# ALPHA x joins the expert rows where they leave PSUM, and two combines sum two gated rows only

## The chip, the cores and the metric

The kernel runs on one core of one Trainium2 chip. The metric is the device time of one execution in microseconds (us). The engines are TensorE (PE, with its weight loads as PEld), VectorE (DVE), ScalarE (ACT), GpSimd (POOL) and SyncE (SP); the last three and the DMA queues also start transfers. All data here are float32.

## What is computed

The reference is one step of a two-layer decoder for 1024 prompt tokens and 8 sample tokens, 1032 rows of D = 1024. Each layer has a mixer (layer 0: RWKV-7 heads and windowed attention; layer 1: causal pooling) and a mixture of 16 experts, of which each token uses two. After both comes a residual with ALPHA and a layer norm:

```python
gates = vals / vals.sum(-1, keepdims=True)          # the two gates of a token sum to 1
for e in range(N_EXPERTS):
    h = jax.nn.silu(xt @ w_gate[e]) * (xt @ w_up[e])
    y = y + dense_gate[:, e:e + 1] * (h @ w_down[e])
...
x = layer_norm(ALPHA * x + h, ln_mix_g, ln_mix_b)   # after the mixer
f = moe_ffn(x, ...)
x = layer_norm(ALPHA * x + f, ln_ffn_g, ln_ffn_b)   # after the experts
```

## The kernel before

The kernel is a row of stages, one after the other, with a barrier of all engines between them: projection and attention, the recurrence, the output projection of layer 0, then twice an expert stage and a combine. Line numbers are those of the kernel before.

**Expert stage** (`experts`, once for each layer). Tokens are sorted by expert into blocks of 128 slots; 22 blocks are worked through in layer 0 and 24 in layer 1. Block j is handled in body j of a loop that every engine runs, two bodies (u = 0, 1) to an iteration; buffers are double, chosen by u. In body j TensorE does, in this order, the gate and up products of block j (L2390), the transposes of the x rows of block j+1 (L2362), the down products of block j-1 (L2373) into PSUM banks 5 and 6, and the transposes of hidden of block j (L2402). ScalarE does Silu (L2455), half of the copy of the transposed x (`xT`, L2435), then `out` for block j-1: columns 0 to 511 of the result from PSUM to `y` (L2445), the start of the store of `y` to `slots_out` in DRAM (L2448); and last the copy of the transposed hidden (`hiddenT`, L2460). VectorE does the product of hidden and up (L2583), the other half of `xT` (L2435), and columns 512 to 1023 of the result (L2578). GpSimd gathers the x rows of block j+1 into `xs` (`ex_x_rows`, L2336) once the transposes of block j-1 have freed the buffer. SyncE loads the experts' weights, 3 MB each. The semaphores that matter: `xt` (x transposed), `ya` and `yv` (the two halves of `y`), `s_st` (a store has landed), `hc` (hiddenT copied), `down_plus_1` (down products done, plus one).

**Pooling combine** (`combine_pool_mix`, stage `cm`, between the layers). It goes over nine tiles of tokens, the tile of 8 samples first. For each tile GpSimd gathers the two expert rows of every token; ScalarE multiplies the first by its gate (L1731); VectorE adds the second with its gate (L1785), adds ALPHA x (L1787), and does the norm in five passes (L1821 to L1848). TensorE then does the band products of the pooling (L1665), a product with the weights (L1682) with ALPHA x added by a matmul with ALPHA times the identity (L1680), and, after a second norm on VectorE, transposes and router products. A step of the loop handles four tiles at different depths: VectorE's second norm of tile s-2, the first of tile s+1; TensorE's band of tile s, products of tile s-1, transposes of tile s-3.

**Final combine** (`combine`, stage `cb`, the end of the kernel). For each of the nine tiles TensorE sums three terms into PSUM: ALPHA x by a matmul with ALPHA times the identity (L2645), and each of the two gathered rows by a matmul with a diagonal matrix of its gates (L2647), for each half of the columns. Each float32 matmul stands as two instructions in the trace. ScalarE makes the diagonals, those of tile i+2 after the root of tile i (L2660). VectorE does the norm of each tile from PSUM, SyncE stores it. Four tiles fit in PSUM.

## Time and profile before

| | us |
|---|---|
| median of 3 runs | 1603.74 |
| lowest and highest | 1598.55, 1604.15 |
| the profiled execution | 1602.93 |
| its span, first to last instruction | 1601.1 |
| TensorE busy | 1440.0 (90%) |
| VectorE busy | 647.0 (40%) |
| ScalarE busy | 365.1 (23%) |
| GpSimd busy | 210.8 (13%) |
| mean granted TensorE clock | 0.932 |

The busy times are means over stages with different limits. The profile also gives a chain of waits, followed back from the last instruction; tables of busy time by stretch, with the clock that TensorE was granted (1.00 is the upper of its two levels, 0.50 the lower); a timeline, in which the brackets at a row's end give the idle time of the engine before it and what ended that; and the packets of each DMA queue in a stretch.

### The profile page before, as it was taken

How to read it: one execution, taken by the hardware profiler on the slowest of the kernel's cores; microseconds unless marked ns; L12 is line 12 of the kernel's file. 1: busy time of each engine (PE TensorE's matmuls, PEld its weight loads, DVE VectorE, ACT ScalarE, POOL GpSimd, SP SyncE). 2: the span in 40 equal slices, each digit the busy share in tenths (PEclk: the TensorE clock that was granted, in tenths of full speed). 3: DMA queues.
4: the chain of work that ended last, by engine and by line, in shares of the span. 5: the costliest groups of instructions: out<-in, count | busy, mean ns of one | idle time of the engine just before them, and what ended most of it. 6: DMA issues, size and time to landing. Idle time of an engine off the chain costs nothing. (4 is left out here: it accounts for less than half of the span.)

```text
span 1601.1 us, 26296 instructions
## 1 busy us (share of the span) xinstructions
PE 1440.0 (90%) x10111; PEld 880.7 (55%) x10112; DVE 647.0 (40%) x1046; ACT 365.1 (23%) x790; POOL 210.8 (13%) x266
## 2 busy tenths in 40 slices
PE   6999999999689998999479999985993799999968
PEld 4666666666588884445234444433983344444423
DVE  1014443367367753866621111115886111111127
ACT  1004444442323321111111111111221111111111
POOL 4000000000434412110010101005000110101040
PEclk8999998999789999999779999995897899999988
DMA  8593000000210013101667888756025788876353
GB/s 205 119 392 131 15 17 23 27 1 0 58 34 4 5 31 117 40 27 57 215 227 271 302 277 303 269 178 224 1 83 184 249 297 279 292 271 227 126 227 117
DMA packets 137055, 236.96 MB, mean 148 GB/s; under 512 B 20178, under 2 KB 100035, under 8 KB 136682
## 3 DMA queue, kind: packets, MB, share of 16 engines
q1 hardware_dynamic: 113458, 151.01, 29.7%
q0 software_dynamic: 16880, 60.49, 10.2%
q10 hardware_dynamic: 6624, 24.12, 3.7%
q8 instruction: 71, 1.16, 0.3%
q14 instruction: 22, 0.18, 0.0%
HBM read 178.92 MB, written 58.21 MB: 148 GB/s over the span
## 5 line engine op out<-in xcount | busy, mean ns | idle before, releaser
L2390 PE MATMUL ex_pb<-ew_w_gate_up,ex_xT 128*128 x736 | 329.1, 600 | 6.2 <-issue 3.7
L502 PE MATMUL pj_pb<-pj_xT,pj_w 128*128 128x348 f32 (+3 forms) x960 | 293.7, 462 | 0.8 <-ACT pj_xT L536 0.8
L502 PEld LDWEIGHTS pj_pb<-pj_xT,pj_w 128*128 128x128 f32 (+1 forms) x960 | 178.1, 188 | 104.2 <-issue 10.0
L2390 PEld LDWEIGHTS ex_pb<-ew_w_gate_up,ex_xT 128*128 128x128 f32 x736 | 137.7, 192 | 164.6 <-issue 163.7
L2373 PE MATMUL ex_pb<-ew_w_down,ex_hiddenT 128*128 x368 | 165.7, 593 | 3.4 <-ACT ex_hiddenT L2460 3.4
L2583 DVE TENSOR_TENSOR ex_hidden<-ex_hidden,ex_pb 128x256 f32<-128x256 f32 x46 | 19.4, 422 | 323.8 <-ACT ex_hidden L2455 323.8
L2373 PEld LDWEIGHTS ex_pb<-ew_w_down,ex_hiddenT 128*128 128x128 f32 x368 | 66.3, 190 | 69.9 <-issue 69.9
L2578 DVE COPY ex_y_rows<-ex_pb 128x512 f32<-128x512 f32 x46 | 31.8, 692 | 134.5 <-PE ex_pb L2373 134.5
L2455 ACT ACTIVATE ex_hidden<-ex_pb 128x256 f32<-128x256 f32 x46 | 17.8, 386 | 260.6 <-PE ex_pb L2390 260.6
L813 DVE SCALAR_TENSOR_TENSOR mixed<-pj_pb,v_mu,mixed 128x347 f32<-128x347 f32 (+3 forms) x42 | 24.0, 572 | 123.0 <-ACT mixed L655 123.0
L2333 POOL COPY ex_tokens_now<-ex_token_of_slot 128x1 uint32 (+1 forms) x48 | 9.6, 201 | 450.3 <-PE ex_pb L2362 398.7
L2362 PEld LDWEIGHTS ex_pb<-k_ident,ex_x_rows 128*128 128x128 f32 x384 | 46.3, 145 | 36.9 <-issue 24.2
L2362 PE MATMUL ex_pb<-k_ident,ex_x_rows 128*128 128x128 f32 x384 | 51.6, 279 | 12.4 <-DMA ex_x_rows<-scratch_x_stored,ex_tokens_now 12.4
L655 ACT ACTIVATE mixed<-pj_pb,pj_one_minus_mu 128x347 f32<-128x347 f32 (+3 forms) x42 | 23.0, 547 | 167.9 <-PE pj_pb L502 167.9
L1990 PE MATMUL mo_pb<-late_rows,projected_qkv 128*128 128x512 f32 x128 | 59.7, 610 | 0.0
L2445 ACT COPY ex_y_rows<-ex_pb 128x512 f32<-128x512 f32 x46 | 27.0, 586 | 136.7 <-PE ex_pb L2373 136.7
L1990 PE MATMUL mo_pb<-mo_w,minus_kk_then_y 128*128 128x512 f32 x128 | 58.1, 593 | 0.0
L2336 POOL DMA_INDIRECT ex_x_rows<-scratch_x_stored,ex_tokens_now x48 | 46.5, 969 | 38.1 <-POOL ex_tokens_now L2333 38.1
L1990 PEld LDWEIGHTS mo_pb<-late_rows,projected_qkv 128*128 128x128 f32 x128 | 25.1, 197 | 31.5 <-issue 31.5
L1682 PE MATMUL cm_pb<-pm_w_pool,cm_pooled 128*128 128x256 f32 (+1 forms) x144 | 41.5, 415 | 0.0
L1990 PEld LDWEIGHTS mo_pb<-mo_w,minus_kk_then_y 128*128 128x128 f32 x128 | 23.6, 190 | 26.3 <-issue 26.3
L2435 ACT COPY ex_xT<-ex_pb 128x512 f32<-128x512 f32 x48 | 28.1, 586 | 38.7 <-PE ex_pb L2362 38.7
(423 smaller groups left out, 2025.4 us busy)
## 6 DMA issues: line engine op xcount, KB each, us to landing
ew_w_gate_up<-in_w_ex_gate SPq DMA_DIRECT2D x32, 1024.0 KB, 6.6
ew_w_gate_up<-in_w_ex_up SPq DMA_DIRECT2D x32, 1024.0 KB, 9.5
ew_w_down<-in_w_ex_down SPq DMA_DIRECT2D x32, 1024.0 KB, 12.5
scratch_slots_out<-ex_y_rows ACTq DMA_DIRECT2D x46, 512.0 KB
scratch_slots_out<-pj_tmp POOLq DMA_DIRECT2D x4, 4096.0 KB
scratch_x_stored<-x_rows SPq DMA_DIRECT2D x16, 512.0 KB
pj_w<-in_w_in SPq DMA_DIRECT2D x7, 1024.0 KB, 8.7
minus_kk_then_y<-in_x_prompt SPq DMA_DIRECT2D x8, 512.0 KB, 5.5
```

The source lines that it names most:

```text
L502: last = nc.tensor.matmul(product(at)[:, 0:tn], w[:, k_slab % NW, k, c0:c0 + mrows], xT[:, k, x0:x0 + tn], start=(k == 0), stop=(k == KD - 1))
L655: nc.scalar.activation(pr[0:mrows, tile, t0:t0 + n], product(at)[:, 1:1 + n], ACT.Identity, scale=omu[0:mrows, tile:tile + 1]).then_inc(s_ ...
L813: last = stt(out=out[:, 0:n_prompt], in0=product(at)[:, 0:n_prompt], scalar=mu, in1=out[:, 0:n_prompt], op0=ALU.mult, op1=ALU.add)
L1682: last = mm(at, feats[:, j % 2, 2 * gi + k, 0:n], pm.w[:, 2 * gi + k, :], start=False, stop=(k == 1))
L1990: last = mm(pb[0:n, 2 * (i % 2) + h, :], lhs(k, i), (w[:, k, 512 * h:512 * h + 512] if k < 4 else w_swa[:, k - 4, 512 * h:512 * h + 512]), ...
L2336: pool.indirect_dma_start(xs[:, u, :], None, io["x_stored"], bass.IndirectOffsetOnAxis(ap=now[:, u:u + 1], axis=0)).then_inc(s_xs[u], 16)
L2362: last = nc.tensor.transpose(pb[:, k // 4, P * (k % 4):P * (k % 4) + P], xs[:, u, P * k:P * k + P], const["ident"][:, :])
L2373: last = mm(pb[:, 5 + half, :], hT[:, u, k, :], w[:, k, 512 * half:512 * half + 512], start=(k == 0), stop=(k == 1))
L2390: last = mm(pb[:, 2 + u, :], xT[:, u, k, :], w[:, k, :], start=(k == 0), stop=(k == KD - 1))
L2435: copy(xT[:, u, 4 * half:4 * half + 4, :], pb[:, half, :].rearrange("p (k t) -> p k t", k=4)).then_inc(q[sem], 1)
L2445: nc.scalar.copy(y[:, u, 0:512], pb[:, 5, :]).then_inc(q["ya"], 1)
L2578: nc.vector.tensor_copy(y[:, u, 512:1024], pb[:, 6, :]).then_inc(q["yv"], 1)
```

## The change

In the expert stage ScalarE first writes ALPHA x of the block's rows into the result's buffer `y`, and VectorE adds both PSUM banks of the down products to it in one instruction of 1024 columns. The stored rows are then ALPHA x + expert(x). Since a token's two gates sum to 1, the gated sum of its two stored rows holds ALPHA x already, and both combines leave that term out. ScalarE's pass waits until the rows are there (`s_xs`) and until the last store from that buffer has landed (`s_st`); this last wait stood at the result copies before. GpSimd's gather waits for the pass too (`alpha_x`), since the pass reads the rows that the gather overwrites.

```diff
@@ combine_pool_mix, VectorE
-                stt(out=r1, in0=r2, scalar=gates[0:n, i, 1:2], in1=r1, op0=ALU.mult, op1=ALU.add).then_inc(q["both"], 1)
-                dve.wait_ge(q["both"], j + 1)
-                stt(out=x_(j), in0=x_(j), scalar=ALPHA, in1=r1, op0=ALU.mult, op1=ALU.add).then_inc(qa["res"], 1)
+                stt(out=x_(j), in0=r2, scalar=gates[0:n, i, 1:2], in1=r1, op0=ALU.mult, op1=ALU.add).then_inc(qa["res"], 1)
@@ experts, GpSimd, before the gather of block j+1
                     pool.wait_ge(q["xt"], j)
+                    pool.wait_ge(q["alpha_x"], j)
@@ experts, TensorE, before the down products
-                        pe.wait_ge(q["ya"], j - 1)
-                        pe.wait_ge(q["yv"], j - 1)
+                        pe.wait_ge(q["y"], j - 1)
@@ experts, ScalarE
             def out(i, u, first):
                 j = 2 * i + u
-                act.wait_ge(q["down_plus_1"], j + 2)
-                if not first:
-                    act.wait_ge(s_st[u], 16 * i)
-                nc.scalar.copy(y[:, u, 0:512], pb[:, 5, :]).then_inc(q["ya"], 1)
-                act.wait_ge(q["ya"], j + 1)
-                act.wait_ge(q["yv"], j + 1)
+                act.wait_ge(q["y"], j + 1)
                 act.dma_start(io["slots_out"][bass.ds(j * P, P), :], y[:, u, :]).then_inc(s_st[u], 16)
             def body(i, u, first):
                 j = 2 * i + u
+                act.wait_ge(s_xs[u], 16 * i + 16)
+                if not first:
+                    act.wait_ge(s_st[u], 16 * i)
+                nc.scalar.activation(y[:, u, :], xs[:, u, :], ACT.Identity, scale=ALPHA).then_inc(q["alpha_x"], 1)
                 act.wait_ge(q["gu"], j + 1)
@@ experts, VectorE, out
                 dve.wait_ge(q["down_plus_1"], j + 2)
-                if not first:
-                    dve.wait_ge(s_st[u], 16 * i)
-                nc.vector.tensor_copy(y[:, u, 512:1024], pb[:, 6, :]).then_inc(q["yv"], 1)
+                dve.wait_ge(q["alpha_x"], j + 1)
+                nc.vector.tensor_tensor(y[:, u, :], y[:, u, :], pb[:, 5:7, :].rearrange("p b n -> p (b n)"), ALU.add)\
+                    .then_inc(q["y"], 1)
@@ combine, TensorE
-            pe.wait_ge(q["alpha"], 1)
...
-                    nc.tensor.matmul(out[0:n, h, :], alpha_i[0:n, 0:n], xr[0:n, i, half], start=True, stop=False)
                     for c in range(2):
                         last = nc.tensor.matmul(out[0:n, h, :], diag[0:n, i % 2, c, 0:n], r[0:n, i, c, half],
-                                                start=False, stop=(c == 1))
+                                                start=(c == 0), stop=(c == 1))
@@ combine, ScalarE
-            nc.scalar.activation(alpha_i[:, :], const["ident"][:, :], ACT.Identity, scale=ALPHA).then_inc(q["alpha"], 1)
```

On ScalarE one body of the expert loop of the kernel before reads as follows, from Silu (`ex_hidden`) to the copy of `hiddenT`; `ex_y_rows` is `y`, and the DMA is the store to `slots_out`.

```order
L2455 ACTIVATE ex_hidden<-ex_pb 128x256
L2433 REGISTER_ALU
L2435 COPY ex_xT<-ex_pb 128x512
L2444 REGISTER_ALU
L2445 COPY ex_y_rows<-ex_pb 128x512
L2448 ISA
L2448 DMA scratch_slots_out<-ex_y_rows 128x1024
L2460 COPY ex_hiddenT<-ex_pb 128x256
```

The same body of the changed kernel, on the same engine (`ex_x_rows` are the gathered rows; line numbers are those of the changed kernel):

```order
L2447 ACTIVATE ex_y_rows<-ex_x_rows 128x1024
L2451 ACTIVATE ex_hidden<-ex_pb 128x256
L2430 REGISTER_ALU
L2432 COPY ex_xT<-ex_pb 128x512
L2440 ISA
L2440 DMA scratch_slots_out<-ex_y_rows 128x1024
L2456 COPY ex_hiddenT<-ex_pb 128x256
```

The pass that writes `y` now stands ahead of Silu, and the copy from PSUM between `xT` and the store is gone from this engine.

On VectorE a steady step of the pooling combine begins as follows in the kernel before: the second norm of one tile (`cm_stats_b`), then the gated sum and the first norm of a later one (`cm_stats_a`).

```order
L1821 BN_STATS cm_stats_b<-cm_pb 128x6 x2
L1824 BN_AGGR cm_stats_b<-cm_stats_b 128x2
L1831 SCALAR_TENSOR_TENSOR x_rows<-cm_pb,cm_stats_b,late_rows 128x1024
L1785 SCALAR_TENSOR_TENSOR cm_expert_rows<-cm_expert_rows,gates 128x1024
L1787 SCALAR_TENSOR_TENSOR x_rows<-x_rows,cm_expert_rows 128x1024
L1821 BN_STATS cm_stats_a<-x_rows 128x6 x2
```

And in the changed kernel:

```order
L1819 BN_STATS cm_stats_b<-cm_pb 128x6 x2
L1822 BN_AGGR cm_stats_b<-cm_stats_b 128x2
L1829 SCALAR_TENSOR_TENSOR x_rows<-cm_pb,cm_stats_b,late_rows 128x1024
L1785 SCALAR_TENSOR_TENSOR x_rows<-cm_expert_rows,gates 128x1024
L1819 BN_STATS cm_stats_a<-x_rows 128x6 x2
```

One pass of 128 x 1024 is gone between the two norms; the rest stands as it did.

## Rows read from the trace of the kernel before

**Rows 1.** The page's chain that ended last, by line, shares of the span.

```profile
PE cb_pb L2647 2%; PE cb_pb L2645 1%; DMA cb_expert_rows<-scratch_slots_out,slots 0%; DVE cb_stats L1821 0%; DVE x_rows L1848 0%; DVE x_rows L1831 0%; POOL cb_expert_rows L2621 0%; DVE cb_stats L1824 0%; POOL cb_eps L2617 0%; DVE cb_stats L1845 0%; POOLq L119 0%
```

**Rows 2.** Busy time by stretch; columns as in its first line.

```profile
core 0: us, PE busy (x) PEld busy (x) DVE busy (x) ACT busy (x) POOL busy (x), PEclk, DMA share, GB/s
830.00:1060.00 230.00, 230.00 (x684) 112.04 (x683) 35.64 (x60) 38.62 (x80) 21.78 (x38) 1.00 0.81 283
...
1112.00:1132.00 20.00, 20.00 (x62) 11.58 (x61) 11.50 (x15) 2.90 (x5) 0.00 (x0) 0.50 0.02 6
1146.30:1190.20 43.90, 43.62 (x328) 39.64 (x328) 42.78 (x61) 14.16 (x24) 0.00 (x0) 1.00 0.01 1
1208.40:1217.00 8.60, 4.42 (x55) 3.62 (x53) 4.48 (x9) 2.74 (x5) 0.00 (x0) 1.00 0.15 61
1544.50:1548.30 3.80, 3.80 (x5) 1.73 (x6) 0.00 (x0) 0.00 (x0) 2.89 (x4) 0.50 0.97 353
1552.00:1593.30 41.30, 41.30 (x96) 16.52 (x94) 33.13 (x48) 7.74 (x23) 5.97 (x7) 0.99 0.49 194
```

**Rows 3.** Timeline of one body of the expert loop, layer 0: start, duration, instruction, idle before.

```profile
910.26 0.34 ACTq L2448 DMA_DIRECT2D scratch_slots_out<-ex_y_rows  x1
...
916.50 0.39 ACT L2455 ACTIVATE ex_hidden<-ex_pb 128x256 f32<-128x256 f32 x1 [5.48 <-PE ex_pb L2390]
...
917.30 0.69 DVE L2435 COPY ex_xT<-ex_pb 128x512 f32<-128x512 f32 x1
...
918.42 0.96 POOL L2336 DMA_INDIRECT ex_x_rows<-scratch_x_stored,ex_tokens_now  x1 [0.81 <-POOL ex_tokens_now L2333]
...
920.75 7.03 PE L2390 MATMUL ex_pb<-ew_w_gate_up,ex_xT 128*128 x16
...
920.83 0.69 DVE L2578 COPY ex_y_rows<-ex_pb 128x512 f32<-128x512 f32 x1 [2.84 <-PE ex_pb L2373]
```

**Rows 4.** Prices: the instructions of L1787, and the timeline row of L1731.

```profile
L1787 DVE SCALAR_TENSOR_TENSOR x_rows<-x_rows,cm_expert_rows x9: 1214/1224/1226, 1089.9 to 1183.2; 128x1024 f32<-128x1024 f32 x8, 8x1024 f32<-8x1024 f32 x1
...
1164.27 1.13 ACT L1731 ACTIVATE cm_expert_rows<-cm_expert_rows,gates 128x1024 f32<-128x1024 f32 x1
```

**Rows 5.** ScalarE's DMA queue: packets, MB, from 1310.2 to 1317.5; then 1533 to 1535.4.

```profile
q10 hardware_dynamic: 142, 0.52, 17.4%
...
q10 hardware_dynamic: 144, 0.52, 54.2%
```

**Rows 6.** Timeline around those two stores, and at the end of the pooling combine.

```profile
1216.92 0.17 DVE L1795 COPY logits<-cm_pb 128x16 f32<-128x16 f32 x1 [2.46 <-PE cm_pb L1709]
1218.44 0.40 SPq L2229 DMA_DIRECT2D ew_w_gate_up<-in_w_ex_gate  x1
...
1310.30 0.34 ACTq L2448 DMA_DIRECT2D scratch_slots_out<-ex_y_rows  x1
...
1533.10 0.34 ACTq L2448 DMA_DIRECT2D scratch_slots_out<-ex_y_rows  x1
1537.09 0.10 POOL L2617 MEMSET cb_eps<- 128x1 f32 x1 [34.86 <-POOLq L119]
```

**Rows 7.** Timeline: the last down products of the expert stage of layer 0.

```profile
1071.26 3.70 PE L2373 MATMUL ex_pb<-ew_w_down,ex_hiddenT 128*128 x8 [1.72 <-ACT ex_hiddenT L2460]
```

**Rows 8.** Timeline of the pooling combine: the ramp on ScalarE, a steady step on TensorE.

```profile
1104.33 0.21 ACT L1747 COPY cm_pooled<-cm_pb 128x64 f32<-128x64 f32 x1 [10.28 <-PE cm_pb L1661]
...
1179.25 0.30 PEld L1665 LDWEIGHTS cm_pb<-pm_band,x_rows 128*128 128x128 f32 x2 [0.16 <-DVE x_rows L1848]
```

**Rows 9.** Timeline of VectorE in the final combine.

```profile
1551.88 1.30 DVE L1821 BATCH_NORM_STATS2 cb_stats<-cb_pb 128x6 f32<-128x512 f32 x2 [19.02 <-PE cb_pb L2647]
...
1555.32 1.28 DVE L1848 SCALAR_TENSOR_TENSOR x_rows<-x_rows,cb_stats,late_rows 128x1024 f32<-128x1024 f32 x1
...
1556.95 1.30 DVE L1821 BATCH_NORM_STATS2 cb_stats<-cb_pb 128x6 f32<-128x512 f32 x2 [0.35 <-issue]
...
1559.92 1.28 DVE L1848 SCALAR_TENSOR_TENSOR x_rows<-x_rows,cb_stats,late_rows 128x1024 f32<-128x1024 f32 x1
...
1596.29 1.27 DVE L1848 SCALAR_TENSOR_TENSOR x_rows<-x_rows,cb_stats,late_rows 8x1024 f32<-8x1024 f32 x1
```

More of the change, by code:

```diff
@@ L1605, in combine_pool_mix @@
         qb = {k: m.sem(f"b_{k}") for k in LN}
-        q = {k: m.sem(k) for k in "eps alpha sel first both wscaled band feats tr cp rp rpc rl ev zero keep".split()}
+        q = {k: m.sem(k) for k in "eps alpha sel first wscaled band feats tr cp rp rpc rl ev zero keep".split()}
         s_r = [m.sem(f"rows{i}") for i in range(TILES)]
@@ L2275, in experts @@
         r = {k: m.sem(f"route_{k}") for k in "mx ex as rk chain lanes blocks sum parts part tokens token_list now tokens_set tab".split()}
-        q = {k: m.sem(k) for k in "gu xt down_plus_1 ht silu h xca xcv hc ya yv loaded stored".split()}
+        q = {k: m.sem(k) for k in "gu xt down_plus_1 ht silu h xca xcv hc alpha_x y loaded stored".split()}
         s_xs = [m.sem(f"x_rows{u}") for u in range(2)]
@@ L2426, in _ @@
             c = entry(pe, 2 * final + (T_SETS + 1), 0, SETS - 1)
-            pe.wait_ge(q["ya"], 2 * final + 1)
-            pe.wait_ge(q["yv"], 2 * final + 1)
+            pe.wait_ge(q["y"], 2 * final + 1)
             down(final, 1, c)
@@ L2600, in combine @@
         diag = m.sb("gate_diagonals", [P, 2, 2, P])
-        alpha_i = m.sb("alpha_ident", [P, P])
         st = m.sb("stats", [P, 2, 18])
@@ L2604, in combine @@
         pb = m.psum("pb", [P, 8, 512])
-        q = {k: m.sem(k) for k in "eps alpha diag res st var root rs g x out".split()}
+        q = {k: m.sem(k) for k in "eps diag res st var root rs g x out".split()}
         s_r = [m.sem(f"rows{i}") for i in range(TILES)]
```

## The prediction

> **What bounds the kernel now.** I read the page's chain of waits first: its end is TensorE alone, in the last stage, the final combine [rows 1]. The table of stretches comes next, since the change touches three kinds of stage. In the expert loops TensorE is busy for 230.00 of 230.00 us at full clock, with VectorE at 36 and ScalarE at 39 us [rows 2]: whatever VectorE and ScalarE do there is free as long as TensorE is not kept waiting. In the steady part of the pooling combine both TensorE (43.62 of 43.9 us) and VectorE (42.78) are full [rows 2], so relief for one of them alone is worth little. In the final combine TensorE is busy for 41.30 of 41.30 us and VectorE for 33.13 [rows 2]. There the reader should see one clear bound, and how near the second engine stands behind it.
>
> **Final combine.** The two alpha matmuls of a tile go; at f32 each is two instructions, so 12 become 8. 96 instructions in 41.30 us [rows 2] are 0.430 us each: TensorE needs 3.44 us for a tile in place of 5.16. VectorE is next. A tile whose data are there takes it from the statistics at 1556.95 to the end of the last pass at 1559.92 + 1.28 = 1561.20 [rows 9], 4.25 us, say 4.28 with the hop to the next tile. So the stage changes its bound and gains 0.9 us a tile, not 1.7. From the start: TensorE begins at 1544.5 as before, since both versions wait there for the gathered rows. Its first instructions run at clock 0.50 [rows 2], the later ones of the first tile at full clock; the four that go are the last four in time, 4 x 0.43 = 1.72 us, so the first statistics start at 1551.88 - 1.72 = 1550.16. The first tile takes 4.72 us on VectorE as before (a table load on ScalarE lies in it: 1551.88 to 1556.60 [rows 9]), the next seven 7 x 4.28 = 30.0, the last 4.2, in all 1589.1 in place of 1596.29 + 1.27 = 1597.56 [rows 9]: **-8.5 us**. Covers: TensorE has a tile ready 3.44 us after its diagonals, which ScalarE makes one tile ahead, so it keeps ahead of 4.28. The gathers are all issued before 1560, so rows come faster than either engine eats them. Had TensorE stayed the bound, the gain would be 9 x 1.72 = 15.5; that end I exclude by VectorE's 4.25.
>
> **Pooling combine.** VectorE loses one pass of 1.224 us on 128 x 1024 for each of nine tiles [rows 4], 11.3 us with hops. Nearly all of it is covered by TensorE. In the ramp ScalarE has idled 10.28 us for TensorE's first band products when it copies them at 1104.33 [rows 8], and from 1112 to 1132 TensorE is busy 20.00 of 20.00 us at clock 0.50 [rows 2]; only the very first tile's chain (gate, sum, norm) stands ahead of TensorE's start, so the whole ramp moves by one pass, -1.25. In the steady steps TensorE waits 0.16 us a step for VectorE's last pass [rows 8], five times: -0.8. The tail has no gathered tile in it. Sum **-2.05 us**, with about 1 us either way from the moment at which the clock rises, which need not move along with the work.
>
> **Expert loops.** Three edits. First, the result leaves PSUM in one VectorE add over 1024 columns, in place of two half copies side by side. It is not in the trace; its neighbours are 1.22 us (three operands, SBUF, [rows 4]) and 1.28 us [rows 9], so 1.25 against 0.69 [rows 3], and everything behind it comes 0.56 us later: the store, and ScalarE's copy of hiddenT, which is queued behind the store. Inside the loop TensorE needs hiddenT only after the next gate/up products (7 us), so this is free. At the end of a layer it is not: the last down products do wait for that copy, 1.72 us [rows 7], and then the last result itself is on the path. Two layers x 2 x 0.56 = **+2.2 us**.
>
> Second, ScalarE gets a pass ALPHA x over 128 x 1024, 1.13 us by the like pass of the pooling combine [rows 4]. ScalarE has idled 5.48 us before Silu at 916.50 [rows 3], so the pass itself fits. But a wait moves with it: y's buffer must be free, so the store of two blocks ago must have landed, and that wait now stands ahead of Silu, where before it stood behind. Queued behind it are Silu, VectorE's product and both copies of xT, and TensorE waits for these. In the block shown, the store is issued at 910.26 + 0.56 = 910.82. VectorE's xT copy ends at 917.99 and TensorE takes it at 920.75 [rows 3]; counted back over Silu and product, Silu may start as late as 919.1, so the pass must start by 917.9: **7.1 us** after the store's issue. What a store takes: a quiet one has its 144 packets through 2.3 us after issue, and its signal shows at most 4.0 us after issue (1533.10 to 1537.09), a hand-over between stages included [rows 5, 6]. Such a hand-over without a transfer is 1217.09 to 1218.44, 1.35 us [rows 6], so the signal comes about 0.35 us after the last packet. Under the weights' traffic the slowest store, issued at 1310.30, has 142 of 144 packets through by 1317.5 [rows 5, 6]. Followed in this way, the 46 stores take 2.3 to 7.5 us, middle about 4.3. With 0.35 us for the signal four of them pass the limit, by 1.8 us in all, or by near nothing if the later issue does not delay the landing. I take **+1 us**; the ends are 0 and, if the whole 1.7 us between last packet and next stage were the signal's own, about 20 us (17 stores over 5.4 us). I stand near the low end because the hand-over has a measured price.
>
> Under load the signal's delay is in no row. The Trainium skill (DMA: Bandwidth & Descriptors, "Latency and other measured facts") gives an HBM access as 0.2 us on average and 2 us at high load, and says that this receipt makes most of a transfer's fixed cost. By its 2 us the limit would be passed by about 27 us in all; the quiet rows here agree with its low figure, and no row shows its high one.
>
> Third, GpSimd's gather into x's buffer waits for the ALPHA x pass as well as for the transposes. The gather at 918.42 [rows 3] fetches the rows that are transposed two blocks after, near 939; even if the pass ends at 919 it starts 1.6 us later and keeps over ten. Free. SP's queue is not moved past anything.
>
> **Sum** against the profiled execution, 1602.93 us (span 1601.1): -8.5 - 2.05 + 2.2 + 1 = -7.35, which gives 1595.6. The median of the runs lies 0.8 above that execution, so on its scale I say **1596**. The covered cases end at 1592 (no store passes, early clock) and 1601 (several more do).
>
> **Rivals.** (a) The wait for the store takes the gain: slower. Mechanism: ScalarE stands at the ALPHA x pass until a late store signals, Silu is late, TensorE idles. It decides from a signal 7.1 us after issue; with 1.7 us between packets and signal it costs 20 us, so 1602.9 - 8.5 - 2.05 + 2.2 + 20 = 1614.6. For it: the slowest stores are already at 7.5 us [rows 5]. Against it: the 0.35 us of quiet stores. Chance 0.14, part of it with a small bill, between 1601 and 1611.
>
> (b) The clock falls in the final combine: slower. TensorE would work 3.44 us and idle 0.84 in every tile. At clock 0.50 a tile costs 8 x 0.86 = 6.9 us, above VectorE's 4.28, and the stage ends at 1544.5 + 9 x 6.9 + 4.2 = 1610.8 in place of 1597.6, so the kernel at 1602.9 + 13.2 - 2.05 + 3.2 = 1617. Against it: at the end of the pooling combine TensorE is busy 4.42 of 8.60 us, half the time, and the clock stays at 1.00 [rows 2]. Chance 0.05. The Trainium skill (TensorE: Matmul & The Clock Gate, "A second HAM failure mode: psum-queue depth-cycling") tells of a kernel whose short idles between groups of matmuls made the clock swing between its two levels, which speaks for this rival; the row at half load speaks against it.
>
> (c) VectorE, not TensorE, sets the step in the pooling combine, and most of the 11.3 us are gained: about 1602.9 - 8.5 - 10 + 3.2 = 1588. For it: TensorE does wait for VectorE in each step. Against it: only 0.16 us [rows 8]. Chance 0.08.
>
> **Chances.** Forecast 0.68, (a) 0.14, (b) 0.05, (c) 0.08, something else 0.05. The range 1591 to 1607 leaves out (b), the dear half of (a) and most of (c). 0.5% of 1603.74 is 8.0 us, about what a measurement of this kernel tells from no change; the forecast lies 0.3 us inside it. So a little under half of the forecast (0.30), (c) and a share of the rest say faster: 0.40. The other part of the forecast and the small bills of (a) say no change: 0.46. Slower: 0.14.
>
> **What would show it.** Final combine: VectorE's statistics every 4.28 us without idle time, TensorE's matmuls in groups of eight with gaps, clock 1.00, and 44.5 us from the first matmul to the last pass in place of 53.1. Pooling combine: no wait of TensorE for x_rows in the steady steps, step 10.8 us in place of 10.97. Expert loops: no TensorE wait for xT or hidden, except in a few blocks. The ends of both layers 1.1 us longer. I am wrong if TensorE idles for ScalarE or VectorE in many blocks, if a clock of 0.50 shows after 1552 in the final combine, or if the pooling steps shrink by a microsecond.

## The result and the profile after

| | before | changed |
|---|---|---|
| median | 1601.14 us (1597.94 to 1604.15, 4 runs) | 1653.37 us (1650.16 to 1667.18, 4 runs) |
| ratio, 95% interval | | 1.0331 [1.0291, 1.0372] |
| span of the profiled execution | 1601.1 | 1654.5 |
| TensorE busy | 1440.0 | 1455.0 |
| VectorE, ScalarE busy | 647.0, 365.1 | 658.2, 382.7 |

The kernel is 3.3% slower; the forecast was 1596 us. The first thing to do with such a result is to cut both spans at the same events: SyncE's first load of expert weights in each layer, and the memsets of `cm_eps` and `cb_eps` that open the two combines. In brackets stands how long TensorE's clock was granted at 0.50 in that stage.

| stage, us | before | changed | difference | forecast |
|---|---|---|---|---|
| ahead of the experts | 783.2 (64.3) | 790.2 (79.1) | +7.0 | 0 |
| experts, layer 0 | 296.9 (40.9) | 316.6 (47.0) | +19.7 | +1.6 |
| pooling combine | 138.4 (53.1) | 137.2 (55.3) | -1.2 | -2.05 |
| experts, layer 1 | 318.6 (38.8) | 354.7 (61.2) | +36.1 | +1.6 |
| final combine | 64.0 (19.6) | 55.7 (24.9) | -8.3 | -8.5 |

So the two combines did what was forecast, and the whole loss lies in the expert loops, +55.8 us where I had +3.2. (The first stage is the same code in both; it had 14.8 us more at clock 0.50, and half of that is its 7 us. All stage lengths, here and below, are read from one profiled execution of each kernel.)

The final combine, VectorE's timeline from the first tile on, answers to [rows 9]:

```profile
1612.94 1.29 DVE L1819 BATCH_NORM_STATS2 cb_stats<-cb_pb 128x6 f32<-128x512 f32 x2 [18.28 <-PE cb_pb L2640]
...
1617.59 1.29 DVE L1819 BATCH_NORM_STATS2 cb_stats<-cb_pb 128x6 f32<-128x512 f32 x2
...
1621.75 1.29 DVE L1819 BATCH_NORM_STATS2 cb_stats<-cb_pb 128x6 f32<-128x512 f32 x2
...
1649.63 1.27 DVE L1846 SCALAR_TENSOR_TENSOR x_rows<-x_rows,cb_stats,late_rows 8x1024 f32<-8x1024 f32 x1
```

Behind the first tile the statistics come every 4.16 us with no idle time in brackets: VectorE is the bound now, as forecast (4.28). The clock was granted at 1.00 from 1612.3 to 1643.0, while TensorE worked 3.67 of every 4.16 us. Then it fell, with half of the last tile still to do:

```profile
1643.00:1651.00 8.00, 2.92 (x4) 0.26 (x2) 7.69 (x12) 0.59 (x2) 0.00 (x0) 0.50 0.33 132
```

The eight matmuls of that tile took 4.98 us in place of 3.67, but VectorE came to it only at 1646.71, after their end, so it cost nothing. The stretches in the expert loop and in the steady part of the pooling combine answer to [rows 2] (stretch, its length, busy time and instructions of PE, PEld, DVE, ACT, POOL, then clock, DMA share, GB/s):

```profile
830.00:1060.00 230.00, 214.90 (x628) 103.29 (x626) 41.98 (x56) 42.48 (x74) 20.64 (x36) 0.99 0.75 261
1174.00:1217.00 43.00, 43.00 (x332) 39.42 (x331) 38.18 (x57) 13.44 (x23) 0.00 (x0) 1.00 0.06 22
```

In the pooling combine TensorE is full and VectorE has slack (38.18 of 43.00 where it had 42.78 of 43.90): the relief of VectorE is worth little there, as forecast. In the expert loop TensorE, which was busy for 230.00 of 230.00 us in the kernel before, has lost 15.1, and got 628 instructions done in place of 684. The page's group of the gate/up products, before and then changed (count, busy, mean ns of one, idle time before them and what ended most of it), says more:

```profile
L2390 PE MATMUL ex_pb<-ew_w_gate_up,ex_xT 128*128 x736 | 329.1, 600 | 6.2 <-issue 3.7
```

```profile
L2389 PE MATMUL ex_pb<-ew_w_gate_up,ex_xT 128*128 x736 | 344.7, 624 | 40.2 <-issue 28.4
```

Idle time ahead of these products went from 6.2 to 40.2 us, and the same 736 instructions are busy 15.6 us longer: 49.6 of the 55.8 us. Most of the idle time is ended by "issue", which is the profile's word for a wait that it cannot put to any other engine or DMA. One body of the loop, layer 0, shows how it comes about. First ScalarE and VectorE:

```profile
936.32 0.34 ACTq L2440 DMA_DIRECT2D scratch_slots_out<-ex_y_rows  x1
936.70 0.37 ACT L2456 COPY ex_hiddenT<-ex_pb 128x256 f32<-128x256 f32 x1 [4.73 <-DVE ex_y_rows L2573]
944.25 1.06 ACT L2447 ACTIVATE ex_y_rows<-ex_x_rows 128x1024 f32<-128x1024 f32 x1 [7.17 <-DMA scratch_slots_out<-ex_y_rows]
945.21 0.37 ACT L2451 ACTIVATE ex_hidden<-ex_pb 128x256 f32<-128x256 f32 x1
...
945.61 0.42 DVE L2579 TENSOR_TENSOR ex_hidden<-ex_hidden,ex_pb 128x256 f32<-128x256 f32 x1 [9.48 <-ACT ex_hidden L2451]
945.95 0.68 DVE L2432 COPY ex_xT<-ex_pb 128x512 f32<-128x512 f32 x1
```

The store goes out at 936.32, the ALPHA x pass can start at 944.25, Silu at 945.21; in [rows 3] Silu stood 6.24 us after the store's issue, here it stands 8.89. By 946.63 the last thing that TensorE's next products need (VectorE's half of `xT`) is there. TensorE itself:

```profile
946.09 0.44 PE L2400 MATMUL ex_pb<-k_ident,ex_hidden 128*128 128x128 f32 x2
949.51 8.82 PE L2389 MATMUL ex_pb<-ew_w_gate_up,ex_xT 128*128 x16 [2.98 <-issue]
```

The transposes of hidden run at 946.09, as soon as hidden is there (945.61 + 0.42 = 946.03). Then TensorE does nothing for 2.98 us, although all its data are in place 0.1 us after the transposes' end. And the products behind the idle time take 8.82 us where they take 7.03 in [rows 3]: the clock, which stood at 1.00, is granted at 0.58 in the mean from 949.5 to 953.0:

```profile
949.50:953.00 3.50, 3.49 (x5) 1.59 (x6) 0.00 (x0) 0.36 (x1) 0.00 (x0) 0.58 0.96 354
```

So the wait for the store is there, as rival (a) had it. But it does not explain 3 us with all data in place. The profile does show what TensorE's sequencer did in that time, if one asks for the lines of the loop and of the table reads and not for the matmuls. The reads of the table of blocks in the changed kernel, in the window 946 to 950 (count, lowest, middle and highest ns of one, first and last start; PEldq is TensorE's sequencer):

```profile
L2287 PEldq TENSOR_LOAD <-block_experts x3: 297/297/299, 946.9 to 948.3; - x3
```

The loop's own instructions stand from 946.09, 0.05 us after hidden is ready, to 946.68; the three reads and what goes with them from 946.73 to 948.93; the waits and the address of the weights from 948.99 to 949.45; and the first weight load at 949.50. The same three reads in the body of [rows 3], kernel before:

```profile
L2289 PEldq TENSOR_LOAD <-block_experts x3: 299/306/308, 917.5 to 918.9; - x3
```

Hidden is ready at 917.34 there, and the sequencer's first instruction behind the wait stands at 917.39; but the array is then still at the down products, until 920.5, so the reads cost nothing. In all 46 bodies of both kernels the sequencer's next instruction comes 0.05 us after hidden is ready.

**The theories.** A: TensorE's own stream stands at its wait for hidden, and what comes next in that stream, the loop's branch and three reads of the table of blocks (which expert, which set of weights), is done only after the wait; it costs about 3 us, which otherwise lie under the queued down products. The rows above speak for it; what a late Silu costs by it, and whether moving the reads takes the cost away, the runs below try. The order of TensorE's instructions in the kernel before, from the last down product into the next body (`block_experts` is the table, L2289 reads it):

```order
L2373 MATMUL ex_pb<-ew_w_down,ex_hiddenT 128x512
L2402 MATMUL ex_pb<-k_ident,ex_hidden 128x128 x2
L2289 ISA
L2289 TENSOR_LOAD block_experts
L2289 ISA x3
L2289 TENSOR_LOAD block_experts
L2289 ISA x2
L2289 TENSOR_LOAD block_experts
L2289 ISA x2
```

B: the lateness of the store, or the DMA traffic, is the whole cost. C: the ALPHA x pass itself is too much for ScalarE.

### The profile page after: what moved, and what is told of

The parts are those of the page before. It is cut to its first block and busy times, and to the rows that moved or that the text cites. A ratio compares the mean times of both kernels' runs of the same rounds, so it can differ in the third digit from the quotient of the medians.

```text
span 1654.5 us, 26187 instructions
## 1 busy us (share of the span) xinstructions
PE 1455.0 (88%) x10075; PEld 884.7 (53%) x10076; DVE 658.2 (40%) x1037; ACT 382.7 (23%) x789; POOL 211.8 (13%) x266
## 5 line engine op out<-in xcount | busy, mean ns | idle before, releaser
L2389 PE MATMUL ex_pb<-ew_w_gate_up,ex_xT 128*128 x736 | 344.7, 624 | 40.2 <-issue 28.4
L2389 PEld LDWEIGHTS ex_pb<-ew_w_gate_up,ex_xT 128*128 128x128 f32 x736 | 142.9, 199 | 211.5 <-issue 210.9
L2447 ACT ACTIVATE ex_y_rows<-ex_x_rows 128x1024 f32<-128x1024 f32 x46 | 48.7, 1058 | 193.0 <-DMA scratch_slots_out<-ex_y_rows 192.8
L2573 DVE TENSOR_TENSOR ex_y_rows<-ex_y_rows,ex_pb 128x1024 f32<-128x1024 f32 x46 | 56.1, 1220 | 93.5 <-PE ex_pb L2372 93.3
L2456 ACT COPY ex_hiddenT<-ex_pb 128x256 f32<-128x256 f32 x46 | 17.2, 373 | 173.6 <-DVE ex_y_rows L2573 173.6
L2640 PE MATMUL cb_pb<-cb_expert_rows,cb_gate_diagonals 128*128 128x512 f32 (+1 forms) x72 | 37.0, 666 | 15.6 <-DMA cb_expert_rows<-scratch_slots_out,slots 12.8
L2451 ACT ACTIVATE ex_hidden<-ex_pb 128x256 f32<-128x256 f32 x46 | 17.5, 380 | 98.0 <-PE ex_pb L2389 98.0
```

The costliest lines, as they stand in the source:

```text
L2389: last = mm(pb[:, 2 + u, :], xT[:, u, k, :], w[:, k, :], start=(k == 0), stop=(k == KD - 1))
L2447: nc.scalar.activation(y[:, u, :], xs[:, u, :], ACT.Identity, scale=ALPHA).then_inc(q["alpha_x"], 1)
L2573: nc.vector.tensor_tensor(y[:, u, :], y[:, u, :], pb[:, 5:7, :].rearrange("p b n -> p (b n)"), ALU.add)\
L2640: last = nc.tensor.matmul(out[0:n, h, :], diag[0:n, i % 2, c, 0:n], r[0:n, i, c, half], start=(c == 0), stop=(c == 1))
```

## Experiments

### The wait alone, the pass alone

`e1_wait_only` is the kernel before with one wait more:

```diff
             def body(i, u, first):
                 j = 2 * i + u
+                if not first:
+                    act.wait_ge(s_st[u], 16 * i)
                 act.wait_ge(q["gu"], j + 1)
```

> The kernel before, with one line more: in the expert loop ScalarE waits ahead of Silu until the store of two blocks ago has landed. No pass, no new add, combines as before. Theory (the wait for a late store holds back Silu): most of the loss of the two expert stages comes back, which was 56 us in the traces (316.6 + 354.7 us in place of 296.9 + 318.7); so about 1601 + 45 = 1646 us (the store starts 0.6 us earlier than in the changed kernel, so a little less than the whole). Rival (the pass, the longer add or the later gather cost the time): 1601 us, within 0.5%.

Measured: 1616.15 us, ratio 1.0083 [1.0048, 1.0119]. `e5_pass_only` has no wait for the store, but 1.24 us of useless work on ScalarE ahead of its wait for the gate/up products, into an unused PSUM bank:

```diff
+                for k in range(2):
...
+                    nc.scalar.activation(pb[:, 7, :].rearrange("p (k t) -> p k t", k=4),
+                                         const["ident"][:, :].unsqueeze(1).to_broadcast([P, 4, P]), ACT.Identity, scale=ALPHA).then_inc(q["own"], 1)
                 act.wait_ge(q["gu"], j + 1)
```

> The kernel before, with an extra pass of the same size on ScalarE ahead of Silu (two passes of 128 x 512 into an idle PSUM bank, unused, each waiting only for the one before on its own engine), and no wait for the store. Theory of the wait: ScalarE idles over 5 us there, so 1601 us within 0.5%. Rival (the pass itself): towards 1650 us.

Measured: 1602.28 us, 0.9996 [0.9967, 1.0025]. The gate/up group of e1, then of e5:

```profile
L2390 PE MATMUL ex_pb<-ew_w_gate_up,ex_xT 128*128 x736 | 331.2, 603 | 14.3 <-issue 11.6
```

```profile
L2390 PE MATMUL ex_pb<-ew_w_gate_up,ex_xT 128*128 x736 | 328.6, 600 | 6.2 <-issue 3.7
```

Theory C falls: a pass of this length that fits into ScalarE's idle time costs nothing. The wait alone costs 13 us, again by "issue", far less than the 45 us that I had expected of it. The other 43 come only with wait and pass together: the pass stands between the store's signal and Silu, and the stores of e1 land no later than those of the kernel before (4 of the 42 that are waited for have their last packet later than 6.75 us after issue, against 5).

### The pass behind Silu; the combines alone

`e3_pass_behind` is the changed kernel with both waits and the pass moved behind Silu and the copy of `xT`. `e4_combines_only` has the combines of the changed kernel and the experts of the kernel before; ALPHA x is left out of both residuals.

```diff
@@ e3, ScalarE (the same lines are gone from the start of body)
                 copy_x(act, nc.scalar.copy, 1 - u, 0, "xca", j + 1)
+                act.wait_ge(s_xs[u], 16 * i + 16)
+                if not first:
+                    act.wait_ge(s_st[u], 16 * i)
+                nc.scalar.activation(y[:, u, :], xs[:, u, :], ACT.Identity, scale=ALPHA).then_inc(q["alpha_x"], 1)
```

> The changed kernel, with ScalarE's ALPHA x pass and its wait for the store moved behind Silu and the copy of xT, and ahead of the start of the store. Same instructions, same sums. Theory of the wait ahead of Silu: the expert stages return to their length before, plus 1.1 us at the end of each; the combines keep their gain of about 9.6 us: 1601 - 9.6 + 2.2 = 1594 us. Rival (the pass, the add over 1024 columns or the gather's extra wait cost the time, wherever the pass stands): 1650 us as the changed kernel.

> The two combines of the changed kernel with the expert stage of the kernel before; ALPHA x is left out of both residuals. The part of the change that gains, alone. Expected from the stage lengths in the two traces (pooling combine -1.2, final combine -8.4): 1601 - 9.6 = 1591.5 us. If the combines' gain were only the other side of a later start, 1601 us.

Measured: e3 1602.41 us, 0.9996 [0.9966, 1.0025]; e4 1585.56 us, 0.9894 [0.9856, 0.9931]. Stages (clock 0.50 in brackets):

| stage, us | before | e4 | e3 |
|---|---|---|---|
| experts, layer 0 | 296.9 | 296.4 | 303.7 |
| pooling combine | 138.4 (53.1) | 127.1 (34.6) | 137.2 (55.3) |
| experts, layer 1 | 318.6 | 318.9 | 324.1 |
| final combine | 64.0 | 55.0 | 55.6 |

e4 is faster than forecast by 6 us, and not by the change: its pooling combine stood at clock 0.50 for 18.5 us less. Where that time is the same as before (e3, the changed kernel) the stage is 1.2 us shorter.

e3 takes 51 us off the changed kernel, so the place ahead of Silu is the loss. It still pays 12.5 us in the experts over e4. 2.2 are the ends of the layers; for the rest see the wait of TensorE's weight loads for gathered rows (total, times, longest), in e4 and then in e3:

```profile
PEld ex_pb L2360 <- DMA ex_x_rows<-scratch_x_stored,ex_tokens_now: 12.6, 2, 6.4
```

```profile
PEld ex_pb L2361 <- DMA ex_x_rows<-scratch_x_stored,ex_tokens_now: 29.7, 20, 6.4
```

The gather waits for the pass, and with the pass behind Silu it comes too late in 18 blocks, 17.1 us of waits at the weight loads. That is my third edit, which I had called free with over ten us of room. I had taken the wrong block: the gather of block j+1 waits for the pass of block j-1. In a steady body a gather was issued 20.7 us ahead of the transposes that need its rows in the kernel before, 9.2 to 17.6 us ahead in the changed kernel, and 5.6 to 9.1 us ahead in e3.

### What a late Silu costs, with no store in it

`e8_silu_late` is the kernel before with the same useless passes, this time between the wait for the gate/up products and Silu. Silu starts 1.53 us after the transposes of x in place of 0.28, so 1.25 us late in every block.

```diff
                 act.wait_ge(q["gu"], j + 1)
                 if not first:
                     act.wait_ge(q["ht"], j - 1)
+                for k in range(2):
...
+                    nc.scalar.activation(pb[:, 7, :].rearrange("p (k t) -> p k t", k=4),
+                                         const["ident"][:, :].unsqueeze(1).to_broadcast([P, 4, P]), ACT.Identity, scale=ALPHA).then_inc(q["own"], 1)
                 nc.scalar.activation(h[:, u, :], pb[:, 2 + u, 0:FF], ACT.Silu).then_inc(q["silu"], 1)
```

> The kernel before, with Silu made late by a fixed amount: ScalarE makes two useless passes of 512 columns behind its wait for the gate/up products, ahead of Silu, in each of the 46 blocks; about 1.2 us. No store is waited for. Theory A: the slack of Silu is under 1 us, so each block pays; with the 0.4 to 1.0 us a block that the stalls of the two earlier runs show for this lateness, 1620 to 1650 us. The slack of 2.6 us of my forecast: no cost, 1601 us.

Measured: 1654.2 us, 1.0309 [1.0286, 1.0332], just the size of the whole loss. Two bodies, TensorE's timeline:

```profile
933.42 0.38 PE L2402 MATMUL ex_pb<-k_ident,ex_hidden 128*128 128x128 f32 x2
934.20 7.13 PE L2390 MATMUL ex_pb<-ew_w_gate_up,ex_xT 128*128 x16 [0.39 <-issue]
...
945.47 0.38 PE L2402 MATMUL ex_pb<-k_ident,ex_hidden 128*128 128x128 f32 x2
946.89 7.13 PE L2390 MATMUL ex_pb<-ew_w_gate_up,ex_xT 128*128 x16 [1.03 <-issue]
```

and VectorE's product that makes hidden, in the same two:

```profile
931.04 0.42 DVE L2588 TENSOR_TENSOR ex_hidden<-ex_hidden,ex_pb 128x256 f32<-128x256 f32 x1 [9.34 <-ACT ex_hidden L2460]
...
943.02 0.42 DVE L2588 TENSOR_TENSOR ex_hidden<-ex_hidden,ex_pb 128x256 f32<-128x256 f32 x1 [8.61 <-ACT ex_hidden L2460]
```

Hidden is ready at 931.46 and 943.44. The transposes of hidden start no later than before (4.31 us after those of x), for they are queued behind the down products. What is late is the next body: its products start 2.74 and 3.45 us after hidden. The first is a body inside an iteration of the loop, the second crosses the loop's branch; all bodies of the run behind the first two of a layer alternate so, with periods (from one block's transposes of x to the next's) of 12.04 and about 12.7 us in place of 11.40 and 11.47. In the body of [rows 3], in the kernel before,

```profile
916.92 0.42 DVE L2583 TENSOR_TENSOR ex_hidden<-ex_hidden,ex_pb 128x256 f32<-128x256 f32 x1 [6.88 <-ACT ex_hidden L2455]
```

hidden is ready at 917.34, and 917.34 + 2.74 = 920.08 against a start at 920.75: a slack of 0.67 us. In bodies with the branch the slack is none (products 3.49 us after hidden, where 3.45 is the least); they last 11.47 and not 11.40 already in the kernel before. `e11_silu_half_as_late` has one useless pass in place of two, as a check on these two figures:

> The kernel before with one useless pass of 512 columns ahead of Silu in place of two, so Silu about 0.6 us late in every block. The run with two passes (1.26 us late) had periods of 12.04 and 12.71 us in turn, in place of 11.40 and 11.47, so a slack of 0.62 us in the blocks inside an iteration of the loop and of none in those at its branch. Expected by that: periods of 11.40 and about 12.1, 23 x 0.6 = 14 us in all, 1616 us. If the cost were proportional (0.94 us a block for 1.26 us), 22 us, 1624; if there were a threshold above 0.6 us, 1602.

Measured: 1622.14 us, 1.0093 [1.0068, 1.0119]. Silu is 0.54 to 0.59 us late, and the periods are 11.40 and 11.96 to 12.03 us, as expected: the bodies with slack pay nothing, the others nearly all. (The stages are 19.6 us longer, 6 more than expected: the way to the second body of each layer, where no down products cover TensorE's stream, pays 3.6 us.)

### TensorE's reads ahead of the wait

To try theory A itself, the transposes of hidden of block j, with their waits, stand behind the table reads of body j+1; the array executes the same instructions in the same order.

```diff
             def body(i, u, first):
                 c = entry(pe, T_SETS + j, 0, SETS - 1)
...
+                if not (first and u == 0):
+                    hidden_turned(i - 1 + u, 1 - u, first)
                 pe.wait_ge(q["xca"], j + 1)
...
                     down(i - 1 + u, 1 - u, c_before)
-                pe.wait_ge(q["h"], j + 1)
...
-                last.then_inc(q["ht"], 1)
```

On e8, `e9_silu_late_reads_first`:

> The same late Silu, with TensorE's transposes of hidden behind the table reads of the next body. Theory A: the slack is 2 to 3 us again, so 1.2 us cost nothing, 1602 us (1594 to 1610). Theory B: as without the move, 1620 to 1650 us.

Measured: 1608.91 us, 1.0033 [1.0012, 1.0054]; e8 without the move took 1654.2. Periods 11.40 us in every body behind the first two, with Silu as late as in e8, and the rows that answer to those of e8, TensorE's two and the reads of the table:

```profile
926.40 0.38 PE L2383 MATMUL ex_pb<-k_ident,ex_hidden 128*128 128x128 f32 x2
926.62 7.03 PE L2401 MATMUL ex_pb<-ew_w_gate_up,ex_xT 128*128 x16
```

```profile
L2289 PEldq TENSOR_LOAD <-block_experts x3: 298/302/305, 921.4 to 922.8; - x3
```

Hidden is ready at 924.44 there; the reads are over by 923.4 and no longer wait for it. (Its control, e7 below, takes 1591.34 us. In the profiled executions e9 has 7.7 us more in the experts, where the way to the second body of each layer takes 13.19 in place of 9.08 us, since no down products cover a late Silu there; and 7.7 us more in the pooling combine, with 18 us more at clock 0.50.)

On the changed kernel, `e6_reads_first`:

> The changed kernel, with one thing moved: TensorE's transposes of hidden of block j, and the waits for hidden ahead of them, stand at the start of body j+1, behind that body's reads of the table of blocks. What the array executes, and in which order, is unchanged. Theory A (a late hidden costs because TensorE's own stream stands at that wait and only then does the loop branch and the table reads, some 3 us, which otherwise lie under the queued down products): the slack of Silu grows to the 2 to 3 us of my forecast, TensorE idles behind the transposes of hidden in a few blocks only, and the time falls from 1653 to about 1597 us (1590 to 1610). Theory B (the lateness of Silu itself is the cost, or the memory traffic is): nothing changes, 1640 to 1655 us.

Measured: 1605.52 us, 1.0006 [0.9983, 1.0030], 48 us below the changed kernel. On the kernel before, as the control, `e7_reads_first_before`, and the same kernel once more beside the last runs, `e7_again`:

> The control: the same move of TensorE's transposes of hidden, on the kernel before. Silu is never late there, so theory A expects no change, 1601 us (1593 to 1609); if the move itself is worth something whatever Silu does, it shows here as 1590 us or less.

> The control again, on the same chip as the version in place: the kernel before with TensorE's transposes of hidden behind the table reads. 1591 us if its 12.6 us gain repeats (3.3 us of it in the expert loops, the rest in a shorter stretch at clock 0.50 in the pooling combine and ahead of the experts); 1599 us if that stretch is a matter of the run.

Measured: 1591.34 us, 0.9921 [0.9896, 0.9947], and 1593.53 us, 0.9930 [0.9904, 0.9956]. I had expected no change. Its experts are 2.3 and 0.8 us shorter (every body 11.40, none 11.47, and the second body of a layer 9.07 in place of 10.34); 7.3 us are the pooling combine, 131.1 (35.5 at clock 0.50) in place of 138.4 (53.1). So the 48 us between e6 and the changed kernel are not a gain that the move brings to any kernel: in the expert stages it takes 43.5 us off the changed kernel and 3.1 off the kernel before.

What e6 still pays is the store. Its experts take 300.9 and 326.9 us against 294.6 and 317.8 in the control, 15.4 us more; about 2 are the ends of the layers, and 12 bodies with a late Silu are 13.0 us over 11.40 in sum (in one of them about 0.9 us is a wait for late gathered rows). One of the two worst in layer 0:

```profile
928.91 1.06 ACT L2453 ACTIVATE ex_y_rows<-ex_x_rows 128x1024 f32<-128x1024 f32 x1 [7.83 <-DMA scratch_slots_out<-ex_y_rows]
...
930.83 0.43 PE L2382 MATMUL ex_pb<-k_ident,ex_hidden 128*128 128x128 f32 x2 [0.61 <-DVE ex_hidden L2585]
931.73 7.13 PE L2400 MATMUL ex_pb<-ew_w_gate_up,ex_xT 128*128 x16 [0.46 <-DVE ex_xT L2438]
```

Here TensorE's waits have names, hidden and xT, and no "issue". In e6 a body whose Silu is x us behind the transposes of x pays about x - 2.56: 3.11 gave 11.93 us, 4.39 gave 13.23, and 2.50 gave 11.40. Less the 0.28 at which Silu stands anyway, that is a slack of 2.3 us; I had counted 2.6.

### Waits taken out of Silu's way

`e12_pass_behind_reads_first` puts both cures together, the pass behind and the reads first:

> The changed kernel with the ALPHA x pass and its waits behind Silu and the copy of xT, and TensorE's transposes of hidden behind the table reads. With the pass behind, the experts took 303.7 and 324.1 us, against 296.4 and 318.9 without ALPHA x; the trace showed TensorE waiting for late gathers (11 us). If that is the rest of the cost, the move of the transposes gives only the 3 to 5 us it gave the kernel before: 1598 us. If the reads were the rest, 1590 us.

Measured: 1604.88 us, 1.0000 [0.9977, 1.0022], 7 us above what I had expected. The median is no better than that of e3. In the profiled execution its experts are 3.4 and 0.6 us shorter (300.3 and 323.5), and the late gathers stay: the waits of the weight loads for them are 30.9 us, 22 times. The rest of the cost of e3 is the gather.

`e10_in_place` takes the cause of both waits away. The result is written over the gathered rows, by one VectorE instruction that also applies ALPHA, and stored from there; the memory of the result's two buffers gives two more for gathered rows, and the wait for a landed store stands on GpSimd, four blocks later. With four buffers an iteration of the loop holds four bodies in place of two.

```diff
-        xs = m.sb("x_rows", [P, 2, D])
-        y = m.sb("y_rows", [P, 2, D])
+        xs = m.sb("x_rows", [P, 4, D])
@@ VectorE, out
+                nc.vector.scalar_tensor_tensor(out=at_(b), in0=at_(b), scalar=ALPHA,
+                                               in1=pb[:, 5:7, :].rearrange("p b n -> p (b n)"),
+                                               op0=ALU.mult, op1=ALU.add).then_inc(q["y"], 1)
@@ GpSimd, before the gather
                     pool.wait_ge(q["xt"], j)
-                    pool.wait_ge(q["alpha_x"], j)
...
+                    pool.wait_ge(s_st[1 - u], 16 * (i + u) - 16)
```

> The changed kernel with no pass and no wait ahead of Silu: the gathered rows have four buffers in place of two, the result's buffers are gone, and VectorE writes ALPHA x + down products over the gathered rows in one instruction of 1024 columns, from where they are stored. The wait for a landed store stands on GpSimd ahead of the gather four blocks on. TensorE's transposes of hidden stand behind the table reads, as in the two runs before. The combines are those of the changed kernel. Theory (both the lateness of Silu and the reads are cured, and the combines keep their gain): the control with the reads first (1591 us) less 8.4 us of the final combine and about 1 of the pooling combine, plus 2.2 at the ends of the layers: 1584 us (1578 to 1592). Rival (the saving in the combines is given back by something else that the fused rows bring): 1591 us or more.

Measured: 1595.2 us (1591.86 to 1598.58, 6 runs), 0.9932 [0.9915, 0.9949]. The gate/up group and the stretch of the expert loop:

```profile
L2408 PE MATMUL ex_pb<-ew_w_gate_up,ex_xT 128*128 x736 | 327.6, 598 | 3.6 <-DVE ex_xT L2446 3.0
```

```profile
830.00:1060.00 230.00, 229.99 (x685) 112.10 (x686) 46.29 (x60) 26.55 (x59) 22.74 (x39) 1.00 0.83 285
```

Nearly every body lasts 11.40 us, and the final combine keeps its gain (54.0 us). It is 8.8 us faster than the kernel before, and no faster than the kernel before with the reads first (1593.53 on the same chip). By the numbers that is the rival of my expectation. The stages of the profiled executions say where the gain of the final combine went: against e7_again that stage is 10.0 us shorter, but the experts are 3.3 and 2.2 longer, and the pooling combine 5.5, for it stood 54.6 us at clock 0.50 where the other stood 35.5. The first 60 us of the pooling combine in three kernels, the kernel before, e7_reads_first_before, and e10:

```profile
1080.00:1140.00 60.00, 42.11 (x185) 30.79 (x186) 37.31 (x45) 10.92 (x17) 22.78 (x23) 0.57 0.42 150
```

```profile
1076.00:1136.00 60.00, 40.17 (x236) 32.80 (x237) 45.36 (x57) 14.31 (x22) 22.79 (x23) 0.75 0.43 150
```

```profile
1083.00:1143.00 60.00, 43.33 (x191) 31.86 (x192) 33.68 (x44) 11.96 (x20) 22.47 (x23) 0.58 0.42 150
```

The mean clock of that stretch is 0.57, 0.75 and 0.58, and TensorE gets 185, 236 and 191 instructions done. In the profiled executions the time at 0.50 is near 35 us (e1, e4, both runs of e7), 42 (e5, e8, e11) or 54 (before, changed, e3, e6, e9, e10, e12). Only e7 has two such executions, and they agree; so even whether this belongs to the kernel or to the execution is open, and no run here was made for it.

## Why the prediction was wrong

**Final combine: right in its mechanism, and in its number with some luck.** -8.3 for -8.5; VectorE became the bound, and rival (b) did not come as far as VectorE had to wait for it: from the first matmul at 1606.09 to the end of the last pass at 1649.63 + 1.27 are 44.8 us (44.5 forecast). Two errors meet in that. The first statistics came 6.85 us after the first matmul, not 5.66, since the clock rose only at 1612.3; from there on the stage took 37.96 us, not 38.9, with a step of 4.16 and not 4.28. And the sign that I had named against myself, a clock of 0.50 in this stage, did show, in the last tile, where it cost nothing.

**Pooling combine: right, with a spread that I had too small.** -1.2 for -2.05 at nearly the same time at clock 0.50. TensorE's first band products came 1.22 us earlier (1.25 forecast), the steady steps took 10.73 us in place of 10.97 with no wait for `x_rows` (10.8 forecast), and the last band products came 1.94 us earlier; 0.75 us was lost again behind them, which I did not follow. But the time at clock 0.50 goes with up to 10 us in the length of this stage between kernels, where I allowed for one. In the profiled executions this stage alone is 10 us shorter than I had expected in e4, which came out 6 us below its expectation, and 6.5 us longer in e10, which came out 11 us above; 3.3 us more are the experts of e10.

**Expert loops, the ends of the layers: right.** +2.2 was forecast. From the start of a layer's last gate/up products to the end of its expert stage are 22.04 and 22.02 us in the kernel before, 22.99 and 22.88 in the changed one: +1.8.

**Expert loops, the store wait: this is the step that failed.** "Counted back over Silu and product, Silu may start as late as 919.1" was the term, and from it came the limit of 7.1 us and the cost of 1 us. I counted back only over the data that TensorE's products need. TensorE's own stream has to get there too: in the steady bodies with a late Silu the products started 2.70 to 2.78 us after hidden, or 3.44 to 3.55 where the loop branches. The slack was 0.67 us and none, not 2.6 (e8, e11, and e9 and e6, in which moving the reads gives it back). The pass stands between signal and Silu, so the pass had to start 5.5 or 4.6 us after the store's issue, by the kind of body, not 7.1, and the middle store has its last packet through only after 4.4. An estimate of what this error alone was worth: with the landing times that I had, those of the kernel before, and 0.43 us for the signal, 21 stores pass these two limits, by 33 us in all. In the changed kernel Silu stands 1.2 us or more behind the transposes of x in 16 of the 42 bodies in which a store is waited for. These last 11.8 to 17.5 us, 55 us over 11.40 in sum. The four with Silu 2.8 to 3.0 us behind last 13.3 to 13.5 us; the nine with 3.1 us and more last 14.9 to 17.5, since behind the idle time the clock fell too in eight of them: 15.6 us of the 55.8 are longer products, a term that my sum did not have.

**Its second part, how late a signal comes, was half right.** The pass that waits for it started 0.4 to 0.65 us behind the store's last packet, for all 84 stores that are waited for in the changed kernel and e6; I had 0.35. But I took the landing times of the kernel before for those of the changed one. There 5 of 42 stores had their last packet later than 6.75 us after issue (I had counted four); in the changed kernel 14 had, in e6 13. With about the limit that I had counted, e6 shows what the term should have been: 12 us, not 1. The store of the body above, ScalarE's DMA queue from 936.3 to 943.9, answers to [rows 5]:

```profile
q10 hardware_dynamic: 144, 0.52, 16.9%
```

All 144 packets are through by 943.9, and the pass starts at 944.25. The Trainium skill (DMA: Bandwidth & Descriptors, "Latency and other measured facts") gives 2 us for an HBM access at high load; the signals here, under 261 GB/s, show nothing of that size behind the last packet. Why the stores land later in the changed kernel is open: they are issued 0.48 us later (6.01 us behind the transposes of x in place of 5.53), and the gathers move too; no run separates the two.

**The gather: wrong, but without effect in the changed kernel.** I took the cover from the wrong block; 9.2 us of it were left, and no transposes waited. It costs where the pass stands later (e3, e12).

**The rivals.** (a) had the mechanism, and its price of 20 us is nearer to what e6 pays for the store (12) than my 1. What made it 56 was in no case of mine. The trace of the kernel before held the hints: 3.7 us of "issue" ahead of the gate/up products, all of it in the second bodies of the two layers, ahead of which no down products run; periods that alternate by 0.07 us; and, plainest, the sequencer's reads that start right behind hidden in every body. A busy time of 230.00 of 230.00 us does not show it: a slack that is just used up leaves no idle time.

The Trainium skill (Perfetto Trace Analysis, "Tensor Engine Instruction (MATMUL, LD_WEIGHTS)") describes that a matmul that waits for a semaphore is put into a wait queue while the sequencer goes on to decode. By that rule the table reads would run while the transposes wait for hidden, and a late Silu would cost nothing up to 2.3 us. The trace does not agree for this stream: in the kernel before the weight load of the transposes carries the wait for hidden itself, and yet the sequencer's next instruction stands 0.05 us after hidden in 46 of 46 bodies; and e8 against e9 is 1654.2 against 1608.9 us. Of the 3.47 us between hidden and the products in the body shown above, 0.65 are the loop's end, 2.2 the three reads, and 0.55 the waits and the address behind them.

## What to carry to other kernels

When a step may be late, count back to its consumer over two paths: the data, and the consumer's own instruction stream, with the register reads, waits and branches that stand between its wait and its next big instruction. An "issue" wait behind an engine's own wait marks such a path, and the profile's rows of the engine's sequencer, asked for by the line of the read or the loop, show when it is worked through; put the reads ahead of the wait, and what waits for a transfer behind what others wait for, or take its cause away with a buffer. And a distribution of landing times read from one kernel holds for that kernel's timing only.

## What the runs showed of the hardware

- TensorE with all its data in place starts its next products 2.74 us after the semaphore it had waited for, with three table reads in between, and 3.45 us with a loop branch too; the profile calls it "issue". A read takes 0.30 us, and with what goes with it the next starts 0.64 to 0.93 us later, 0.75 in the middle. Its sequencer did not run ahead of a weight load that waits for another engine (46 of 46 bodies).
- In the expert loops of the changed kernel TensorE idled nine times for 1.97 to 2.99 us ahead of the gate/up products. With eight of these the clock fell to 0.50, and the 16 instructions behind took 8.6 to 10.1 us in place of 7.03; with one, of 2.98 us, it stayed, and they took 7.13. It stayed as well with the eight idle times of 1.06 to 1.84 us (a layer's first body apart, which starts at 0.50).
- In the final combine, with TensorE at work 3.67 of every 4.16 us, the clock stayed at 1.00 for 30.7 us and fell before the end of the last tile; in the kernel before, with TensorE full, it fell 0.7 us before the end of TensorE's work.
- The stay at clock 0.50 at the start of the pooling combine was 35, 42 or 54 us in kernels that do nearly the same there, worth up to 10 us of 1600: more than most changes to this kernel bring.
- ScalarE's pass started 0.4 to 0.65 us behind the last packet of the store that it waited for, whether the store took 2.3 or 8.4 us.
